# Six places for the split weights, and a reordered turn from the mixer into the feed-forward part, in a decoder layer on one core

## The chip, the cores and the metric

The kernel runs on one core of a Trainium2 chip. The metric is the device time of one execution in microseconds; less is better.

## The reference, cut to what matters

One layer of a decoder with 256 tokens of width 1024, in float32:

```
h = RMSNorm(x);  columns = h @ w_in          # 1024 x 5400: queries, keys, values, three merge gates
three attention branches -> o_nsa, o_moba, o_mem
merged = sum_i sigmoid(gate_i) * (o_i @ w_i)
y  = merged @ w_mix_out
x1 = x + RMSNorm(y)
h2 = RMSNorm(x1)
out = x1 + RMSNorm((silu(h2 @ w_gate) * (h2 @ w_up)) @ w_down)     # width 2816
```

## The kernel before, in words

Every projection is made from float32 values cut into a high and a low part. A product of two such values takes three matmuls: high times high, high activations times low weights, low activations times high weights. The weights are cut on the chip. They arrive in `raw` (four slots of 1 MB, one slot is one *unit*), and each half of a unit is one *sub*, numbered v. For each sub ScalarE (ACT) rounds 128x1024 values into `wh` (`hi`, L467) and VectorE (DVE) subtracts to get `wl` (`lo`, L756). Then TensorE (PE) runs 12 matmuls of 512 columns on it (`sub`, L1126): two token tiles t, two slices s of the contraction, three products (L1122 to L1124), into the PSUM bank pair `acc` of one block. Four subs make a block, `V_GATE`, `V_NSA`, `V_MIX`, `V_GU` and `V_DOWN` are the first subs of the stages, and `B_...` are the blocks.

`wh` and `wl` have four places (`SUBS`). So `hi` of sub v waits until the matmuls of sub v-4 are done (`mm_done`), and ACT's and DVE's programs name a lead of three subs (`AHEAD`): before each other piece of work they write `hi_to(v_last + AHEAD)` and `lo_to(...)`, which emit all splits up to that sub. The queues of the engines run in the order of the program, so a split that waits holds what stands behind it. The SP engine only issues the loads of `raw`; a slot is free when its two `lo` are done.

The stages in order are: five projection blocks and the memory block (the front); the loop over 24 attention *jobs* (`for n in range(JOBS + 2)`), which gives each job a gate sub, scores, a softmax through ACT, DVE and GpSimd (POOL), `turn` (transposes of the probabilities) and `values`; the output projections of the branches; the blocks `B_MIX` and `B_MIX + 1`, which are the two column halves of `merged @ w_mix_out`; the 11 blocks of gate and up; and down.

Around the change the work is serial by nature. The merged values `yb` come out of DVE (L949); PE transposes them in banks of four 128x128 blocks (`merged_banks`, two banks a call), ACT rounds a bank into `xh` (`round_hi(2, j)`, L506), and DVE makes `xl` (`round_lo(2, j)`, L798). Sub i of `B_MIX` needs bank i. After `B_MIX + 1` each token tile t goes through: sum of squares (ACT L672), root (L518), reciprocal (DVE L1037), two residual adds of 512 columns (`add_residual`, L1044, each gives `x1_done[n]`), transposes of the new x (`new_x_bank(t, n)`, L1202), `round_hi(3, 2t + n)` on ACT (L500) and `round_lo(3, 2t + n)` on DVE (L791), which give `th_done` and `tl_done`. The first feed-forward block `B_GU` is run by `by_tiles`: all of tile 0, then all of tile 1, and each pair of subs waits for `tl_done`, which is the low part. The square of the new x for the second norm (L696) comes after all roundings, for both tiles at once, followed by the load of the Silu table (L700).

Of the kernel before, what the change touches and what calls it, by code (L numbers as in the profile page):

```python
# [25 lines left out]
F32 = mybir.dt.float32  # L26
# [31 lines left out]
RAW, SUBS = 4, 4  # L58
AHEAD = SUBS - 1
# [6 lines left out]
V_GATE, V_MOBA, V_MEM, V_GATE_NSA, V_NSA, V_MIX, V_GU, V_DOWN = 24, 40, 42, 44, 52, 56, 2 * U_GU, 2 * U_DOWN  # L66

# [43 lines left out]

def look_ahead(n):

    return AHEAD - 1 if n < 6 else AHEAD


def build_layer(nc, a, out, g_scratch):
# [13 lines left out]
    with ExitStack() as ctx:  # L131
# [77 lines left out]
        with late:  # L209
            ah = sb("ah", [P, KF, SEQ], F32R, late)  # L210
            al = sb("al", [P, KF, SEQ], F32R, late)
            yb = sb("yb", [P, TILES, D], F32, late)
            tmp = sb("tmp", [P, TILES, SLICE], F32, late)
# [239 lines left out]
        def _(act):  # L453
# [7 lines left out]
            def hi(v, slot, half, w, first_load):  # L461

                act.wait_ge(loaded[slot], first_load)
                if not (isinstance(v, int) and v < SUBS):
                    act.wait_ge(mm_done, v - SUBS + 1)
                k = (2 * slot + half) % SUBS
                nc.scalar.activation(wh[:, k, :, 0:w], raw[:, slot, 2 * half:2 * half + 2, 0:w], ACT.Copy).then_inc(hi_done, 1)  # L467

            def first_hi(k):
# [7 lines left out]
                nc.scalar.activation(wh[:, k // 2, k % 2], raw[:, k // 4, k % 4], ACT.Copy).then_inc(hi_done, 1)  # L477

            def hi_to(v_end):
                while split[0] <= min(v_end, 2 * UNITS - 1):  # L480
                    v = split[0]
                    u = v // 2
                    hi(v, u % RAW, v % 2, width(v), 32 * (u // RAW + 1))
# [40 lines left out]
            split[0] = SUBS  # L524
# [11 lines left out]
            def evac_cols(b):  # L536
                v_last = 4 * b + 3
                hi_to(v_last + AHEAD)
# [90 lines left out]
            for n in range(JOBS + 2):  # L629
                hi_to(V_GATE + n + AHEAD)  # L630
# [47 lines left out]
            hi_to(V_MIX + 7)  # L678
# [3 lines left out]
            hi_to(V_GU + 1)  # L682
            round_hi(3, 0)
            hi_to(V_GU + 2)
# [16 lines left out]

            def ffn_hi(i, j, s):

                v = V_GU + AHEAD + s + 4 * i
                vj = AHEAD + s + 4 * j
                hi(v, (vj // 2) % RAW, vj % 2, SLICE, ((V_GU + vj) // 2 // RAW + 1) * 32 + (i - j) * 16)
# [6 lines left out]
            def ffn_act(i, j, first):  # L713
                for s in range(4):
                    if not first:
                        ffn_hi(i, j, s)
                    if s == 2 and not first:
# [12 lines left out]
            ffn_act(0, 0, True)  # L730
            with nc.scalar.Fori(0, (GU_BLOCKS - 1) // 2) as it:
                for j in range(2):
                    ffn_act(it * 2 + (1 + j), 1 - j, False)
            split[0] = V_GU + 4 * GU_BLOCKS + AHEAD
            hi_to(V_DOWN + 2 + AHEAD)
            ffn_ah(GU_BLOCKS - 1)
            nc.scalar.preload_act_table(ACT.Sqrt)
            for n in range(2):
                v_last = V_DOWN + 11 * n + 10
                hi_to(v_last + AHEAD)  # L740
# [8 lines left out]
        def _(dve):  # L749
            split = [0]  # L750

            def lo(v, slot, half, w):

                dve.wait_ge(hi_done, v + 1 + SUBS)
                k = (2 * slot + half) % SUBS
# [3 lines left out]
            def first_lo(k):  # L759

                dve.wait_ge(hi_done, k + 1)
                nc.vector.tensor_tensor(wl[:, k // 2, k % 2], raw[:, k // 4, k % 4], wh[:, k // 2, k % 2].bitcast(F32),
                                        ALU.subtract).then_inc(lo_done, 1)

            def lo_to(v_end):
                while split[0] <= min(v_end, 2 * UNITS - 1):
                    v = split[0]
                    lo(v, v // 2 % RAW, v % 2, width(v))
# [51 lines left out]
            split[0] = SUBS  # L820
# [18 lines left out]
            def evac_cols(b):  # L839
                v_last = 4 * b + 3  # L840
                lo_to(v_last + AHEAD)
# [210 lines left out]
            lo_to(V_MIX + 7)  # L1052
# [17 lines left out]
            lo_to(V_GU + AHEAD + 3)  # L1070
            dve.wait_ge(root_done, 5)
            reciprocals(3, 3)
            dve.wait_ge(rstd_done, 5)

            def ffn_lo(i, j, s):
                vj = AHEAD + s + 4 * j
                lo(V_GU + AHEAD + s + 4 * i, (vj // 2) % RAW, vj % 2, SLICE)
# [6 lines left out]
            def ffn_dve(i, j, first):  # L1084
                for s in range(4):
                    if not first:
                        ffn_lo(i, j, s)
                    if s == 2 and not first:
# [8 lines left out]
            ffn_dve(0, 0, True)  # L1097
            with nc.vector.Fori(0, (GU_BLOCKS - 1) // 2) as it:
                for j in range(2):
                    ffn_dve(it * 2 + (1 + j), 1 - j, False)  # L1100
            split[0] = V_GU + 4 * GU_BLOCKS + AHEAD
            lo_to(V_DOWN + 2 + AHEAD)
            ffn_al(GU_BLOCKS - 1)
            dve.wait_ge(gpostd, 32)
            lo_to(V_DOWN + 10 + AHEAD)
# [12 lines left out]
        def _(pe):  # L1118
# [7 lines left out]
            def sub(v, slot, parity, h, l, k0, w, first, last):  # L1126

                pe.wait_ge(lo_done, v + 1 + SUBS)
                for t in range(TILES):
# [3 lines left out]
                    if t == 0 and last:  # L1133
                        ins.then_inc(acc0_done, 1)
                ins.then_inc(mm_done, 1)
# [8 lines left out]
            def whole_block(b, v0, subs, h, l, k0=0, w=SLICE, ready=None, after=None):  # L1144
# [3 lines left out]
                for i in range(subs):  # L1148
                    if ready is not None:
                        ready(i)  # L1150
                    sub(v0 + i, (v0 + i) % SUBS, b % 2, h, l, k0 + 2 * i, w, i == 0, i == subs - 1)
# [3 lines left out]
            def first_block(after):  # L1155

                for k in range(PIECES):
                    slot, s = k // 2, k % 2
# [16 lines left out]
            def by_tiles(b, v0, subs, h, l, k0, ready=None, after=None, first=True):  # L1175
# [3 lines left out]
                for t in range(TILES):  # L1179
                    for i in range(subs):  # L1180
                        v = v0 + i
                        if t == 0:
                            pe.wait_ge(lo_done, v + 1 + SUBS)
# [327 lines left out]
```

## Time and profile before

| what | value |
|---|---|
| median of 3 runs | 421.06 us (418.35 to 421.47) |
| the profiled execution | 418.43 us, its span 416.6 us |
| PE busy | 408.3 us, 98% of the span |
| DVE / ACT / POOL busy | 260.9 / 234.0 / 32.1 us |
| granted TensorE clock | 1.00 in this execution |
| moved by DMA | 78.82 MB, mean 189 GB/s |

A busy share counts a matmul from its start to its modelled end, and these overlap. So the share doesn't show a short bubble; the distance from one start to the next does.

### The profile page before, as it was taken

How to read it: one execution, taken by the hardware profiler on the slowest of the kernel's cores; microseconds unless marked ns; L12 is line 12 of the kernel's file. 1: busy time of each engine (PE TensorE's matmuls, PEld its weight loads, DVE VectorE, ACT ScalarE, POOL GpSimd, SP SyncE). 2: the span in 40 equal slices, each digit the busy share in tenths (PEclk: the TensorE clock that was granted, in tenths of full speed). 3: DMA queues.
4: the chain of work that ended last, by engine and by line, in shares of the span. 5: the costliest groups of instructions: out<-in, count | busy, mean ns of one | idle time of the engine just before them, and what ended most of it. 6: DMA issues, size and time to landing. Idle time of an engine off the chain costs nothing.

```text
span 416.6 us, 5880 instructions
## 1 busy us (share of the span) xinstructions
PE 408.3 (98%) x2070; PEld 328.6 (79%) x2070; DVE 260.9 (63%) x454; ACT 234.0 (56%) x402; POOL 32.1 (8%) x72
## 2 busy tenths in 40 slices
PE   9999999999999999999999999999999999999994
PEld 5787789877777777778787788888888888888883
DVE  4854865875766789756859665555555655545434
ACT  5653964577767766745546774444554454545321
POOL 3210020021212121210000000000000000000000
PEclk9999999999999999999999999999999999999999
DMA  8999993535344335367654467555655556655002
GB/s 295 392 335 368 376 338 114 192 108 196 109 151 146 101 102 169 136 220 238 198 178 171 132 225 229 169 173 189 201 187 168 170 183 199 202 203 197 6 0 101
DMA packets 52016, 78.82 MB, mean 189 GB/s; under 512 B 2076, under 2 KB 28488, under 8 KB 51992
## 3 DMA queue, kind: packets, MB, share of 16 engines
q1 hardware_dynamic: 50216, 73.52, 53.4%
q0 software_dynamic: 1344, 4.43, 3.2%
q10 hardware_dynamic: 432, 0.56, 0.4%
q8 instruction: 14, 0.23, 0.2%
q14 instruction: 10, 0.08, 0.1%
HBM read 77.43 MB, written 1.07 MB: 188 GB/s over the span
## 4 chain that ended last, share of the span: by engine, by line
PE 96%; DVE 1%; ACT 1%; issue 1%; DVEq 0%; ACTq 0%
PE acc L1122 27%; PE acc L1124 27%; PE acc L1123 27%; PE ob L1363 3%; PE sbank L1312 3%; PE ptb L1326 2%; PE ptb L1445 1%; PE ptb L1282 1%; PE acc L1161 1%; PE acc L1165 1%; PE acc L1166 1%; PE sbank L1233 1%; DVE xl L791 1%; ACT xh L500 0%; PE ob L1249 0%
## 5 line engine op out<-in xcount | busy, mean ns | idle before, releaser
L756 DVE TENSOR_TENSOR wl<-raw,wh 128x1024 fp32r<-128x1024 f32 (+1 forms) x126 | 151.4, 1208 | 94.8 <-ACT wh L467 94.3
L467 ACT ACTIVATE wh<-raw 128x1024 fp32r<-128x1024 f32 (+1 forms) x126 | 130.9, 1045 | 91.3 <-PE acc L1124 79.4
L1122 PE MATMUL acc<-wh,xh 128*128 128x512 f32 (+1 forms) x368 | 146.2, 397 | 1.2 <-DVE xl L791 1.2
L1124 PE MATMUL acc<-wh,xl 128*128 128x512 f32 (+1 forms) x368 | 142.2, 387 | 0.0
L1123 PE MATMUL acc<-wl,xh 128*128 128x512 f32 (+1 forms) x368 | 142.0, 386 | 0.0
L1122 PEld LDWEIGHTS acc<-wh,xh 128*128 128x128 f32 x368 | 69.1, 188 | 18.1 <-issue 4.9
L1124 PEld LDWEIGHTS acc<-wh,xl 128*128 128x128 f32 x368 | 69.1, 188 | 14.2
L1123 PEld LDWEIGHTS acc<-wl,xh 128*128 128x128 f32 x368 | 69.2, 188 | 12.6
L1122 PE MATMUL acc<-wh,ah 128*128 128x512 f32 x88 | 34.3, 390 | 0.0
L1124 PE MATMUL acc<-wh,al 128*128 128x512 f32 x88 | 34.3, 389 | 0.0
L1123 PE MATMUL acc<-wl,ah 128*128 128x512 f32 x88 | 34.2, 389 | 0.0
L440 POOL TENSOR_SCALAR sx<-sx,jst 128x256 f32<-128x256 f32 (+1 forms) x48 | 20.3, 436 | 94.4 <-DVE jst L991 52.6
L642 ACT ACTIVATE sx<-sx,jst 128x128 f32<-128x128 f32 (+1 forms) x40 | 17.9, 450 | 8.1 <-DVE jst L981 8.1
L1122 PEld LDWEIGHTS acc<-wh,ah 128*128 128x128 f32 x88 | 16.5, 188 | 3.4
L1123 PEld LDWEIGHTS acc<-wl,ah 128*128 128x128 f32 x88 | 16.5, 188 | 3.4
L1124 PEld LDWEIGHTS acc<-wh,al 128*128 128x128 f32 x88 | 16.5, 188 | 3.4
L726 ACT ACTIVATE silu<-acc,rstd 128x256 f32<-128x256 f32 x22 | 10.4, 476 | 11.8 <-DVE act_tok L1094 8.0
L971 DVE TENSOR_TENSOR sx<-sbank,tb 128x128 f32<-128x128 f32 (+1 forms) x40 | 12.4, 352 | 5.2 <-PE sbank L1312 4.3
L1094 DVE SCALAR_TENSOR_TENSOR act_tok<-acc,rstd,silu 128x256 f32<-128x256 f32 x22 | 10.5, 480 | 6.8 <-ACT silu L726 6.8
L620 ACT ACTIVATE pts<-ptb 128x512 f32<-128x512 f32 x16 | 9.5, 597 | 9.0 <-PE ptb L1326 8.9
L1122 PE MATMUL acc<-wh,oh 128*128 128x512 f32 x32 | 13.0, 405 | 0.0
L672 ACT ACTIVATE tmp<-acc 128x512 f32<-128x512 f32 x8 | 4.8, 600 | 14.2 <-PE acc L1124 14.2
(187 smaller groups left out, 401.7 us busy)
## 6 DMA issues: line engine op xcount, KB each, us to landing
raw<-in_w_in SPq DMA_DIRECT2D x18, 1024.0 KB
raw<-in_w_ffn_gate SPq DMA_DIRECT2D x22, 512.0 KB
raw<-in_w_ffn_up SPq DMA_DIRECT2D x22, 512.0 KB
raw<-in_w_ffn_down SPq DMA_DIRECT2D x22, 512.0 KB
raw<-in_w_mix_out SPq DMA_DIRECT2D x4, 1024.0 KB
raw<-in_w_mem_kv SPq DMA_DIRECT2D x2, 1024.0 KB
raw<-in_w_nsa_o SPq DMA_DIRECT2D x2, 1024.0 KB
raw<-in_w_in SPq DMA_DIRECT2D x3, 512.0 KB, 7.4
```

The costliest lines, as they stand in the source:

```text
L440: ins = nc.gpsimd.tensor_scalar(sx[:, n % 2, lo:hi], sx[:, n % 2, lo:hi], jst[:, 4, n, t:t + 1], 1.0, ALU.mult, ALU.mult)
L467: nc.scalar.activation(wh[:, k, :, 0:w], raw[:, slot, 2 * half:2 * half + 2, 0:w], ACT.Copy).then_inc(hi_done, 1)
L642: ins = nc.scalar.activation(sx[:, n % 2, lo:hic], src[:, n % 2, lo:hic], ACT.Exp, bias=jst[:, 1, n, t:t + 1], scale=SCALE, accum_out=jst[ ...
L726: nc.scalar.activation(silu[:, t], acc[:, j % 2, t, 0:GU_W], ACT.Silu, scale=rstd[:, 3, t:t + 1]).then_inc(silu_done, 1)
L756: nc.vector.tensor_tensor(wl[:, k, :, 0:w], raw[:, slot, 2 * half:2 * half + 2, 0:w], wh[:, k, :, 0:w].bitcast(F32), ALU.subtract).then_in ...
L971: nc.vector.tensor_tensor(sx[:, n % 2, c0:c1], sbank[:, n % 2, c0:c1], tb[:, bh, c1 - c0 - 1::-1], ALU.add).then_inc(dve_c, 1)
L1094: nc.vector.scalar_tensor_tensor(act_tok[:, t], acc[:, j % 2, t, GU_W:2 * GU_W], rstd[:, 3, t:t + 1], silu[:, t], ALU.mult, ALU.mult).then ...
L1122: nc.tensor.matmul(bank[:, 0:w], h[:, k, c], wh[:, slot, s, 0:w], start=first, stop=False)
L1123: nc.tensor.matmul(bank[:, 0:w], h[:, k, c], wl[:, slot, s, 0:w], start=False, stop=False)
L1124: return nc.tensor.matmul(bank[:, 0:w], l[:, k, c], wh[:, slot, s, 0:w], start=False, stop=last)
L1312: ins = nc.tensor.matmul(sbank[:, side, c0:c1], qt[half_rows(side), q, P * t:P * t + P], kt[half_rows(side), k, 0:c1 - c0], start=True, st ...
L1363: ins = nc.tensor.matmul(ob[half_rows(side), c0:c1], v, p, start=(i == 0), stop=(i == count - 1))
```

## The change

It has four parts.

1. `wh` and `wl` get six places. A sub's place is now `ring(v)`, and `hi` waits for the last user of that place, v-6, up to the first feed-forward blocks. The lead stays at three in the front, grows to five over the first jobs, and goes back to four places and three subs from feed-forward block 3 on. For that, feed-forward blocks 1 and 2 are taken out of ACT's and DVE's loops and written out, with fewer splits in them. In the front, after block 1, the splits that are emitted ahead of the copy out of the bank go to sub 9 and not to sub 10.
2. In `B_MIX` the second pair of merged banks is turned in the middle of sub 1 (after its tile 0), and not after sub 0.
3. `B_GU` is written out as `first_ffn_block`. The two products with the high part of the new x run first for a pair of subs, and the product with the low part after them. The high products wait for `th_done` only. The transposes of tile 1 stand after `high(0, 2)` and after `high(1, 0)`.
4. The squares of the new x are made per tile, each ahead of the rounding of one bank of tile 1. On DVE the first residual add of tile 1 now comes before `round_lo(3, 1)`.

The buffer `tmp` shares its memory with `silu` and `act_tok` to make room.

```diff
-RAW, SUBS = 4, 4
-AHEAD = SUBS - 1
+RAW, SUBS, FFN_SUBS, IN_PIECES = 4, 6, 4, 4
+FRONT_AHEAD, AHEAD, FFN_AHEAD = 3, SUBS - 1, FFN_SUBS - 1
+FFN_PARTS = [[V_GU + 9, V_GU + 10, V_GU + 11, V_GU + 12], [V_GU + 13, V_GU + 14]]
+def ring(v):
+    w = v - V_GU
+    return w % SUBS if w < 2 * SUBS else w % FFN_SUBS
+def last_user(v):
+    return v - SUBS if v - V_GU < 2 * SUBS + FFN_SUBS else v - FFN_SUBS
 def look_ahead(n):
-    return AHEAD - 1 if n < 6 else AHEAD
+    return min(AHEAD, max(FRONT_AHEAD - 1, n - 1))
+def hi_look_ahead(n):
+    return min(AHEAD, max(FRONT_AHEAD, n))
+def front_look_ahead(b):
+    return FRONT_AHEAD - 1 if b == 1 else FRONT_AHEAD
...
 # ACT
-                hi_to(v_last + AHEAD)
+                hi_to(v_last + front_look_ahead(b))
...
-                hi_to(V_GATE + n + AHEAD)
+                hi_to(V_GATE + n + hi_look_ahead(n))
...
-            hi_to(V_MIX + 7)
+            hi_to(V_GU + 1)
             squares(0, 1, 0, B_MIX + 1, V_MIX + 7)
             act.wait_ge(sum_done, 1)
             roots(2, 0, 1)
-            hi_to(V_GU + 1)
+            hi_to(V_GU + 3)
             round_hi(3, 0)
-            hi_to(V_GU + 2)
+            hi_to(V_GU + 4)
             squares(0, 1, 1, B_MIX + 1, V_MIX + 7)
             round_hi(3, 1)
             act.wait_ge(sum_done, 2)
             roots(2, 1, 2)
-            hi_to(V_GU + 3)
-            for j in (2, 3):
-                round_hi(3, j)
-            hi_to(V_GU + AHEAD + 3)
-            for n in range(2):
-                act.wait_ge(x1_done[n], 2)
+            hi_to(V_GU + 5)
+            def x_squares(t):
+                for n in range(2):
+                    act.wait_ge(x1_done[n], t + 1)
+                nc.scalar.activation(yb[:, t], xs[:, t], ACT.Square, accum_out=ssq[:, 3, t:t + 1]).then_inc(ssq_done, 1)
             for t in range(TILES):
-                nc.scalar.activation(yb[:, t], xs[:, t], ACT.Square, accum_out=ssq[:, 3, t:t + 1]).then_inc(ssq_done, 1)
+                x_squares(t)
+                round_hi(3, 2 + t)
             act.wait_ge(ssq_done, 6)
             roots(3)
+            hi_to(V_GU + AHEAD + 3)
             nc.scalar.preload_act_table(ACT.Silu)
...
 # DVE
-            lo_to(V_GU + 1)
+            lo_to(V_GU + 3)
             round_lo(3, 0)
-            lo_to(V_GU + 2)
+            lo_to(V_GU + 4)
             sum_halves(0, 1)
             gain(0, 1, 1, B_MIX)
-            round_lo(3, 1)
             norm(1, 4, 2, 4)
             add_residual(0, 1, 0, 2, x1_done)
-            lo_to(V_GU + 3)
+            round_lo(3, 1)
             add_residual(0, 1, 1, 2, x1_done)
-            for j in (2, 3):
-                round_lo(3, j)
-            lo_to(V_GU + AHEAD + 3)
+            round_lo(3, 2)
+            lo_to(V_GU + 5)
+            round_lo(3, 3)
             dve.wait_ge(root_done, 5)
             reciprocals(3, 3)
+            lo_to(V_GU + AHEAD + 3)
...
 # PE
             whole_block(B_MIX, V_MIX, 4, xh, xl, ready=lambda i: pe.wait_ge(tl_done, i + 1),
-                        after={0: [lambda: merged_banks(2, 4)]})
+                        between={1: lambda: merged_banks(2, 4)})
...
-            by_tiles(B_GU, V_GU, 4, xh, xl, 0, ready=4, after={(0, 2): [lambda: new_x_bank(1, 0)], (0, 3): [lambda: new_x_bank(1, 1)]})
+            def first_ffn_block():
+                def high(t, i):
+                    pe.wait_ge(th_done, 4 + 2 * t + i // 2 + 1)
+                    if t == 0:
+                        pe.wait_ge(lo_done, V_GU + i + 1 + IN_PIECES)
+                    for s in range(2):
+                        x = xh[:, 2 * i + s, P * t:P * t + P]
+                        nc.tensor.matmul(acc[:, B_GU % 2, t], x, wh[:, i, s], start=(i == 0 and s == 0), stop=False)
+                        nc.tensor.matmul(acc[:, B_GU % 2, t], x, wl[:, i, s], start=False, stop=False)
+                def low(t, i):
+                    pe.wait_ge(tl_done, 4 + 2 * t + i // 2 + 1)
...
+                for i in range(2):
+                    high(0, i)
+                for i in range(2):
+                    low(0, i)
+                high(0, 2)
+                new_x_bank(1, 0)
+                high(0, 3)
+                low(0, 2)
+                low(0, 3)
+                for half in range(2):
+                    for i in (2 * half, 2 * half + 1):
+                        high(1, i)
+                        if i == 0:
+                            new_x_bank(1, 1)
+                    for i in (2 * half, 2 * half + 1):
+                        low(1, i)
```

## Rows read from the trace of the kernel before

**Rows 1.** The page, section 1: busy time of the engines.

```profile
PE 408.3 (98%) x2070; PEld 328.6 (79%) x2070; DVE 260.9 (63%) x454; ACT 234.0 (56%) x402; POOL 32.1 (8%) x72
```

**Rows 2.** Busy time by stretch: the jobs, then the feed-forward loop; granted clock, DMA share, GB/s.

```profile
84.00:184.00 100.00, 100.00 (x578) 76.81 (x577) 72.84 (x186) 67.59 (x154) 20.80 (x48) 1.00 0.43 138
250.00:350.00 100.00, 100.00 (x460) 82.75 (x459) 56.13 (x61) 49.11 (x61) 0.00 (x0) 1.00 0.60 187
```

**Rows 3.** The waits of PE: us in total, times, longest.

```profile
PE acc L1122 <- DVE xl L791: 1.2, 2, 0.7
...
PE ptb L1207 <- DVE yb L949: 0.2, 1, 0.2
```

**Rows 4.** The timeline at `B_MIX`: start, duration, engine, line, operation, idle before.

```profile
201.77 0.39 PE L1124 MATMUL acc<-wh,xl 128*128 128x512 f32 x1
...
202.40 0.66 PE L1207 MATMUL ptb<-const,yb 128*128 128x128 f32 x4 [0.25 <-DVE yb L949]
...
203.25 0.48 PE L1122 MATMUL acc<-wh,xh 128*128 128x512 f32 x1
...
203.79 0.76 DVE L798 SCALAR_TENSOR_TENSOR xl<-ptb,xh 128x256 fp32r<-128x256 f32 x2 [0.30 <-ACT xh L506]
```

**Rows 5.** The timeline of PE at the end of `B_MIX + 1`, in `B_GU`, and the start of block 1.

```profile
223.08 0.39 PE L1124 MATMUL acc<-wh,xl 128*128 128x512 f32 x1
...
224.14 0.47 PE L1122 MATMUL acc<-wh,xh 128*128 128x512 f32 x1 [0.68 <-DVE xl L791]
...
230.36 0.60 PE L1202 MATMUL ob<-const,xs 128*128 128x128 f32 x4
...
231.44 0.50 PE L1122 MATMUL acc<-wh,xh 128*128 128x512 f32 x1 [0.48 <-DVE xl L791]
...
237.00 0.39 PE L1122 MATMUL acc<-wh,xh 128*128 128x512 f32 x1
```

**Rows 6.** The timeline of ACT in the same stretch.

```profile
221.70 1.14 ACT L500 ACTIVATE xh<-sbank,gx 128x128 fp32r<-128x128 f32 x4 [0.69 <-PE sbank L1202]
...
224.23 1.17 ACT L500 ACTIVATE xh<-sbank,gx 128x128 fp32r<-128x128 f32 x4
...
236.86 1.04 ACT L696 ACTIVATE yb<-xs 128x1024 f32<-128x1024 f32 x1
...
239.38 1.28 ACT L700 ACT_TABLE_LOAD   x1
```

**Rows 7.** The timeline of DVE in the same stretch.

```profile
222.87 1.12 DVE L791 SCALAR_TENSOR_TENSOR xl<-sbank,gx,xh 128x128 fp32r<-128x128 f32 x4 [0.43 <-ACT xh L500]
...
226.94 0.75 DVE L1044 SCALAR_TENSOR_TENSOR xs<-yb,rstd,xs 128x512 f32<-128x512 f32 x1
...
228.74 0.75 DVE L1044 SCALAR_TENSOR_TENSOR xs<-yb,rstd,xs 128x512 f32<-128x512 f32 x1
```

**Rows 8.** The timeline in the front: the first transposes, then sub 12.

```profile
32.38 0.41 PE L1233 MATMUL sbank<-const,pat 128*128 128x128 f32 x2 [0.42 <-issue]
...
39.72 1.06 ACT L467 ACTIVATE wh<-raw 128x1024 fp32r<-128x1024 f32 x1 [5.12 <-DMA raw<-in_w_in]
...
40.81 1.23 DVE L756 TENSOR_TENSOR wl<-raw,wh 128x1024 fp32r<-128x1024 f32 x1 [5.83 <-ACT wh L467]
...
42.19 0.47 PE L1122 MATMUL acc<-wh,xh 128*128 128x512 f32 x1
```

**Rows 9.** The timeline in jobs 4 and 5.

```profile
93.47 1.07 ACT L467 ACTIVATE wh<-raw 128x1024 fp32r<-128x1024 f32 x1
...
96.23 0.93 POOL L440 TENSOR_SCALAR sx<-sx,jst 128x256 f32<-128x256 f32 x2 [3.25 <-DVE jst L994]
...
98.46 0.48 ACT L642 ACTIVATE sx<-sbank,jst 128x256 f32<-128x256 f32 x1
...
99.14 0.60 PE L1326 MATMUL ptb<-const,sx 128*128 128x128 f32 x4
...
101.11 1.13 PE L1312 MATMUL sbank<-kt,qt 64*128 64x256 f32 x8
```

More of the change, by code:

```diff
@@ L212, in build_layer @@
             yb = sb("yb", [P, TILES, D], F32, late)
-            tmp = sb("tmp", [P, TILES, SLICE], F32, late)
+            with ExitStack() as early:
+                tmp = sb("tmp", [P, TILES, SLICE], F32, early)
             silu = sb("silu", [P, TILES, GU_W], F32, late)
@@ L476, in first_hi @@
                     act.wait_ge(loaded[k // 4], 32)
-                nc.scalar.activation(wh[:, k // 2, k % 2], raw[:, k // 4, k % 4], ACT.Copy).then_inc(hi_done, 1)
+                nc.scalar.activation(wh[:, ring(k // 2), k % 2], raw[:, k // 4, k % 4], ACT.Copy).then_inc(hi_done, 1)
             def hi_to(v_end):
@@ L523, in _ @@
                 first_hi(k)
-            split[0] = SUBS
+            split[0] = IN_PIECES
             def squares_of(i, src, t):
@@ L711, in ffn_ah, with ffn_act @@
                 nc.scalar.activation(ah[:, bass.ds(i * 2, 2), :], ptb[:], ACT.Copy).then_inc(ah_done, 1)
-            def ffn_act(i, j, first):
+            def ffn_act(i, j, first, parts=None):
                 for s in range(4):
-                    if not first:
+                    if parts is None:
                         ffn_hi(i, j, s)
+                    elif s < len(parts):
+                        hi_to(parts[s])
                     if s == 2 and not first:
@@ L819, in _ @@
                 first_lo(k)
-            split[0] = SUBS
+            split[0] = IN_PIECES
             dve.wait_ge(bias_row, 1)
@@ L1082, in ffn_al, with ffn_dve @@
                                         ah[:, bass.ds(i * 2, 2), :].bitcast(F32), ALU.subtract).then_inc(al_done, 1)
-            def ffn_dve(i, j, first):
+            def ffn_dve(i, j, first, parts=None):
                 for s in range(4):
-                    if not first:
+                    if parts is None:
                         ffn_lo(i, j, s)
+                    elif s < len(parts):
+                        lo_to(parts[s])
                     if s == 2 and not first:
@@ L1124, in product, with sub @@
                 return nc.tensor.matmul(bank[:, 0:w], l[:, k, c], wh[:, slot, s, 0:w], start=False, stop=last)
-            def sub(v, slot, parity, h, l, k0, w, first, last):
-                pe.wait_ge(lo_done, v + 1 + SUBS)
+            def sub(v, slot, parity, h, l, k0, w, first, last, between=None):
+                pe.wait_ge(lo_done, v + 1 + IN_PIECES)
                 for t in range(TILES):
@@ L1134, in sub @@
                         ins.then_inc(acc0_done, 1)
+                    if t == 0 and between is not None:
+                        between()
                 ins.then_inc(mm_done, 1)
@@ L1142, in free_acc, with whole_block @@
                     pe.wait_ge(ev[t], b - 1)
-            def whole_block(b, v0, subs, h, l, k0=0, w=SLICE, ready=None, after=None):
+            def whole_block(b, v0, subs, h, l, k0=0, w=SLICE, ready=None, after=None, between=None):
                 free_acc(b)
@@ L1150, in whole_block @@
                         ready(i)
-                    sub(v0 + i, (v0 + i) % SUBS, b % 2, h, l, k0 + 2 * i, w, i == 0, i == subs - 1)
+                    sub(v0 + i, ring(v0 + i), b % 2, h, l, k0 + 2 * i, w, i == 0, i == subs - 1, (between or {}).get(i))
                     for work in (after or {}).get(i, ()):
@@ L1414, in _ @@
                 free_acc(b)
-                sub(v, v % SUBS, b % 2, oh, ol, 4, SLICE, True, False)
+                sub(v, ring(v), b % 2, oh, ol, 4, SLICE, True, False)
                 if n == 0:
@@ L1426, in _ @@
-            by_tiles(B_GU, V_GU, 4, xh, xl, 0, ready=4, after={(0, 2): [lambda: new_x_bank(1, 0)], (0, 3): [lambda: new_x_bank(1, 1)]})
+            def first_ffn_block():
[9 more added lines that the diff above has]
+                    pe.wait_ge(tl_done, 4 + 2 * t + i // 2 + 1)
+                    for s in range(2):
+                        ins = nc.tensor.matmul(acc[:, B_GU % 2, t], xl[:, 2 * i + s, P * t:P * t + P], wh[:, i, s], start=False,
+                                               stop=(i == 3 and s == 1))
+                    if t == 1:
+                        ins.then_inc(mm_done, 1)
+                    elif i == 3:
+                        ins.then_inc(acc0_done, 1)
+                for i in range(2):
[14 more added lines that the diff above has]
+                        low(1, i)
@@ L1447, in ffn_turn_at @@
                 ins.then_inc(at_done, 1)
+            free_acc(B_GU)
+            first_ffn_block()
             ffn_body(1, 1, True)
```

76 lines of the change are left out of this document (39 added, 37 removed).

## The prediction

> **What bounds the kernel now.** I read the busy times first: PE has 98% of the span, and DVE and ACT have a third or more of theirs free [rows 1]. Then I asked by stretch: in the jobs and in the feed-forward loop PE is covered for the whole 100 us at a granted clock of 1.00 (the 2.4 GHz level), DMA engines are at 43% and 60% of their time, and DVE has at least 27 us of every 100 free [rows 2]. So the time is the number of PE instructions times their spacing, plus the bubbles. The change removes no PE instruction; it can only take bubbles. The spacing is worked out from rows 5: from the first matmul of tile 1 of `B_GU` at 231.44 to the first of the next block at 237.00 there are 24 matmuls, 5.56 us; the first after transposes lasts 0.50 and not 0.39 and costs those 0.11 more, so one takes (5.56 - 0.11) / 24 = 0.227 us. A full share in a busy column hides bubbles, so the view that matters is that of PE's own waits. It is short: 1.2 us in two waits for the low part of the new x, and 0.2 us for the merged values [rows 3]. No wait of PE for a split weight (`wh`, `wl`) is in that view, in the jobs or after them.
>
> **The bubbles and their sizes**, as start minus previous start minus the normal spacing:
>
> - `B_MIX`: the last matmul of sub 0 starts at 201.77, the transposes at 202.40: 0.63 - 0.23 = 0.40 us [rows 4].
> - `B_GU`, tile 0: from 223.08 to 224.14, 1.06 - 0.23 = 0.83 us [rows 5].
> - `B_GU`, tile 1: the four transposes start at 230.36, the next matmul at 231.44. Eight transposes held PE from 202.40 to 203.25 [rows 4], so four take 0.43 us, and the bubble is 1.08 - 0.43 = 0.65 us [rows 5].
> - The front: PE's sequencer idles 0.42 us ahead of the transposes at 32.38 [rows 8].
>
> The first three add up to 1.88 us, or 0.45% of the span.
>
> **Part by part.**
>
> *Merged banks amid sub 1: takes 0.40 us.* Sub 0 now ends at 201.77 + 0.23 = 202.00, and six matmuls of sub 1 run until 203.36. `yb` was there for transposes at 202.40, so they don't wait. Then eight transposes (0.85), then six more matmuls with 0.11 of restart: sub 2 wants to start at 203.36 + 0.85 + 1.47 = 205.68. It needs `xl` of bank 2, which came at 203.79 + 0.76 = 204.55, that is 2.15 us after the first transpose [rows 4]; now 203.36 + 2.15 = 205.51. The margin is 0.17 us. If it is missed, the loss is at most 0.3 us.
>
> *High parts first: takes 0.83 us.* With the 0.40 from above, `B_MIX + 1` ends at 223.31 - 0.40 = 222.91. The rounding of bank 0 ended at 221.70 + 1.14 = 222.84 [rows 6], now 222.44, so the high products don't wait. Eight of them last until 224.72. The low part of bank 0 came at 222.87 + 1.12 = 223.99 [rows 7], now 223.59, so the low products don't wait either (to 225.63). The high part of bank 1 came at 224.23 + 1.17 = 225.40 [rows 6], now 225.0: margin 0.6 us.
>
> *Transposes of tile 1 and order on DVE: takes 0.65 us.* After `high(0, 2)` PE is at 226.54 and wants `x1_done[0]` of tile 1. Its add started at 226.94 and took 0.75 [rows 7], but one `round_lo` (1.12) stood before it, which now stands behind: 227.69 - 0.40 - 1.0 = 226.3. Margin 0.25 us. The transposes (226.54) are followed by four high and four low products (to about 228.9). ACT meanwhile has the root, one split (1.07), one `x_squares` (1.04 [rows 6]) and `round_hi(3, 2)` (1.14): 225.1 + 1.07 + 1.04 + 1.14 = 228.35. Margin 0.55 us. The second half of the chain is looser: the add of the other columns, with `round_lo(3, 1)` before it, is done near 228.0 (it ended at 229.49 [rows 7]) for transposes at 229.8; `round_hi(3, 3)` is done near 231.5 for 232.2. So I have PE through `B_GU` at 222.91 + 48 x 0.227 + 2 x (0.43 + 0.10) = 234.9, where it was 237.0 [rows 5]. That is 2.1 us; the three bubbles give 1.88, the rest is the slow restart behind each of them. I take 2.0.
>
> *Squares per tile.* Two operations of 1.04 us that stood at 236.86 to 238.9, ahead of the 1.28 us table load at 239.38 [rows 6], now run inside the block. ACT's last splits before the table are bound to PE's subs 0 to 2 of `B_GU`; the third is done at about 235.6, the table at 236.9, Silu of block 0 after it. PE asks for the products two subs into block 1 (234.9 + 5.4 = 240.3). Covered by 2 us; worth nothing by itself.
>
> *Six places.* In the steady state `hi(v)` stands one lead further on and waits for v-6, so it is the same event of PE as before (lead 3, v-4; lead 5, v-6: both are the sub before the current one). ACT and DVE do the same work at the same moments, and only PE's distance grows, by two subs or 5.4 us. PE didn't wait for weights [rows 3], so this gives nothing. It costs where the lead grows: jobs 4 and 5 each have one more `hi` (1.07 us [rows 9]) and, around them, one more `lo` (1.23 us [rows 8]) ahead of the softmax steps. The slack there: POOL's scaling of job 4 ended at 96.23 + 0.93 = 97.16, and PE's transposes of it start at 99.14, so 2.0 us, of which one `hi` takes 1.1. The exponentials of job 5 end at 98.46 + 0.48 = 98.94, and the next scores overwrite their bank at 101.11, so 2.2 us, of which two `hi` take 2.1 less the 0.7 that ACT waited in between: about 1 us is left [rows 9]. The extra splits therefore lie beside PE's work; bounds 0 and, if `hi` and `lo` add up in series, 2 x 2.3 = 4.6 us less the slacks 2.0 + 2.2, so 0.4 us, or 4.6 us if no slack holds. I take 0. A load of `raw` is asked for seven subs ahead of its use both before and after, as both ends move together; the DMA rows have room [rows 2]. Splits that the feed-forward blocks 1 and 2 no longer have were done before; nobody is short there. Code written out for two blocks on ACT and DVE: no row prices it; between 0 and one idle of PE like the 0.42 us of rows 8. I take 0, as those engines are a third free.
>
> At this place the Trainium skill, SBUF — State Buffer, section "SBUF: two separate sides", has a rule against the change: a VectorE operation with two SBUF inputs and a GpSimd operation that reads SBUF shut each other out for a whole instruction. No row here shows POOL beside a `lo`, since POOL starts right after DVE's reciprocal. If an added `lo` did hold POOL in job 4, one of 1.23 us would outlast the 0.9 us of slack left by 0.3 us, and the sum would be 1.7 and not 2.0.
>
> *The front.* Copying block 1 out ahead of sub 10's split lets the transposes at 32.38 start without the 0.42 us idle. But sub 12 waits for its load: `hi` starts at 39.72 behind 5.12 us of waiting for DMA, `lo` ends at 40.81 + 1.23 = 42.04, and PE starts at 42.19 [rows 8]. That load doesn't depend on the splits, so PE arrives earlier and waits longer. Worth 0; up to 0.6 if the load comes earlier too.
>
> **The sum.** 418.43 - 2.0 = 416.4 for an execution like the profiled one (span 414.6; the rest of 1.8 us stays). The profiled one lies at the low end of the runs; the median is 421.06, and against it the forecast is 421.06 - 2.0 = **419.1 us**.
>
> **The rivals.**
>
> - *Part of it comes back* (0.14): the chain of tile 1 has margins of 0.17, 0.25 and 0.55 us. If DVE or ACT are late there by the length of one operation (1.1 us), PE waits at `new_x_bank(1, 0)` or `high(1, 0)`; 1.0 us is left, 420.1. For it: a chain of eight hand-overs. Against it: all durations are from rows.
> - *The lead covers late weights* (0.10): two of three runs took 3 us more than the profiled one, and no trace shows where. If it is a split or a load that comes late after the front, 5.4 us more distance hides it: 418.43 - 2.0 = 416.4 for every run. Against it: the tightest loads are in the front [rows 8], where the lead stays.
> - *The jobs pay* (0.08): in jobs 4 and 5 the added splits stand ahead of exponentials and reciprocals on queues in order. It decides once they delay POOL or the exponentials by more than the 2.0 and 2.2 us of slack. With no slack 4.6 us are lost and 2.0 won: 421.06 + 2.6 = 423.7, slower.
> - *It doesn't do what it says* (0.06): a wait in `B_GU` is inherited from elsewhere, and the freed time is lost before block 1: 421.1.
>
> The forecast itself has 0.62.
>
> **How the numbers follow.** About 1% (4.2 us) is what a measurement here can tell from no change, and the whole sum is half of that. Faster by over 1% needs under 416.9: the second rival and a share of the scatter, 0.10. Slower by over 1% needs over 425.3: only the far end of the third rival, 0.03. Within 1%: 0.87. The range reaches from 416.2 (second rival) to 420.9 (above the first rival, short of the fourth), which leaves out the third and fourth and a little of the scatter of 3 us between runs.
>
> **What would show it.** In the changed profile: PE's waits have no entry for `xl` in `B_GU` over 0.2 us and none for `yb`; first matmul of block 1 about 2 us earlier; the bubble at 32.38 gone and a larger one at 42.19; the squares of x between the roundings of tile 1; POOL and PE in jobs 4 and 5 as before within 0.3 us. It is wrong if PE stands in the new block for `x1_done` or `th_done`, or if a wait of PE turns up in the jobs.

## The result, and the profile after

| kernel | runs | median us | lowest to highest |
|---|---|---|---|
| before | 6 | 419.48 | 418.35 to 421.47 |
| changed | 6 | 416.27 | 416.18 to 416.33 |

The ratio is 0.9915, with a 95% interval of 0.9888 to 0.9942: the change takes 0.85%. The few long runs of the kernel before weigh in the ratio and hardly in a median; the ratio of the medians is 0.9923. The profiled execution took 416.27 us with a span of 414.5 us, against 418.43 and 416.6. So trace against trace it takes 2.1 us, and median against median 3.2 us. Two things have to be explained: that the 2.1 us are where they were forecast, and that the scatter of the kernel before doesn't show in these six runs.

The changed kernel's page, busy time of the engines, and then its waits of PE (us in total, times, longest), which answer to [rows 1] and [rows 3]:

```profile
PE 407.3 (98%) x2070; PEld 328.2 (79%) x2070; DVE 260.6 (63%) x454; ACT 233.1 (56%) x402; POOL 32.9 (8%) x72
```

```profile
PE ptb L1314 <- DVE eps L838: 0.9, 1, 0.9
PE acc L1152 <- DVE wl L782: 0.4, 1, 0.4
PE acc L1193 <- ACT wh L498: 0.2, 1, 0.2
```

The waits for `xl` and for `yb` are gone. A new one for a split weight has come; it is at sub 12 in the front (below). The wait of 0.2 us at L1193 is in the first block, and the one at L1314 was there before. The timeline of the changed kernel at `B_MIX`, answering to [rows 4]:

```profile
203.24 0.39 PE L1154 MATMUL acc<-wh,xl 128*128 128x512 f32 x1
203.48 0.60 PE L1239 MATMUL ptb<-const,yb 128*128 128x128 f32 x4
...
204.27 0.48 PE L1152 MATMUL acc<-wh,xh 128*128 128x512 f32 x1
...
204.80 0.76 DVE L824 SCALAR_TENSOR_TENSOR xl<-ptb,xh 128x256 fp32r<-128x256 f32 x2 [1.21 <-ACT xh L527]
...
205.50 0.39 PE L1154 MATMUL acc<-wh,xl 128*128 128x512 f32 x1
...
205.73 0.40 PE L1152 MATMUL acc<-wh,xh 128*128 128x512 f32 x1
```

The last matmul of tile 0, the transposes and the next matmul follow each other with no idle time noted. From the last matmul of sub 1 at 205.50 to the first of sub 2 at 205.73 is 0.23, the normal spacing; `xl` of bank 2 was ready at 204.80 + 0.76 = 205.56.

`B_GU` in the same timeline, answering to [rows 5] and [rows 6]:

```profile
222.74 0.39 PE L1154 MATMUL acc<-wh,xl 128*128 128x512 f32 x1
...
222.97 0.40 PE L1466 MATMUL acc<-wh,xh 128*128 128x512 f32 x1
...
226.04 1.08 ACT L715 ACTIVATE yb<-xs 128x1024 f32<-128x1024 f32 x1
...
226.39 0.39 PE L1467 MATMUL acc<-wl,xh 128*128 128x512 f32 x1
226.62 0.60 PE L1234 MATMUL ptb<-const,xs 128*128 128x128 f32 x4
226.98 0.48 PE L1466 MATMUL acc<-wh,xh 128*128 128x512 f32 x1
...
227.26 1.14 ACT L521 ACTIVATE xh<-ptb,gx 128x128 fp32r<-128x128 f32 x4
...
228.91 0.40 PE L1466 MATMUL acc<-wh,xh 128*128 128x512 f32 x1
```

Where PE stood 0.83 us beyond its spacing there is now the spacing alone, 222.97 - 222.74 = 0.23. Tile 1's transposes start one spacing after the matmul before them, and hold PE for 226.98 - 226.62 = 0.36 us. `round_hi(3, 2)` ends at 227.26 + 1.14 = 228.40, and `high(1, 0)` starts at 228.91, right after the low products. Block 1 then starts here:

```profile
233.93 1.07 PE L1472 MATMUL acc<-wh,xl 128*128 128x512 f32 x4
...
234.84 0.39 PE L1152 MATMUL acc<-wh,xh 128*128 128x512 f32 x1
```

It was 237.00 [rows 5], so 2.16 us earlier, which is all of the difference of the spans (2.1). The front, answering to [rows 8]:

```profile
32.02 0.38 PE L1265 MATMUL sbank<-const,pat 128*128 128x128 f32 x2
...
39.69 1.06 ACT L488 ACTIVATE wh<-raw 128x1024 fp32r<-128x1024 f32 x1 [5.49 <-DMA raw<-in_w_in]
...
41.38 0.39 PE L1154 MATMUL acc<-wh,xl 128*128 128x512 f32 x1
...
42.16 0.47 PE L1152 MATMUL acc<-wh,xh 128*128 128x512 f32 x1 [0.38 <-DVE wl L782]
```

The bubble before the transposes is gone, the one at sub 12 is 42.16 - 41.38 - 0.23 = 0.55 us, and sub 12 starts at 42.16 where it was 42.19. Jobs 4 and 5, answering to [rows 9]:

```profile
93.44 2.02 ACT L488 ACTIVATE wh<-raw 128x1024 fp32r<-128x1024 f32 x2
...
97.14 0.93 POOL L462 TENSOR_SCALAR sx<-sx,jst 128x256 f32<-128x256 f32 x2 [4.19 <-DVE jst L1020]
...
98.00 2.35 DVE L782 TENSOR_TENSOR wl<-raw,wh 128x1024 fp32r<-128x1024 f32 x2
...
99.20 0.60 PE L1358 MATMUL ptb<-const,sx 128*128 128x128 f32 x4
...
101.19 0.49 PE L1344 MATMUL sbank<-kt,qt 64*128 64x256 f32 x2
```

Two splits stand where one stood. POOL starts 0.91 us later than at 96.23 [rows 9], and PE's transposes come at 99.20 where they came at 99.14.

### The profile page after: what moved, and what is told of

The parts are those of the page before. It is cut to its first block, busy times and chain, and to the rows that moved or that the text cites. A ratio compares the mean times of both kernels' runs of the same rounds, so it can differ in the third digit from the quotient of the medians.

```text
span 414.5 us, 5854 instructions
## 1 busy us (share of the span) xinstructions
PE 407.3 (98%) x2070; PEld 328.2 (79%) x2070; DVE 260.6 (63%) x454; ACT 233.1 (56%) x402; POOL 32.9 (8%) x72
## 4 chain that ended last, share of the span: by engine, by line
PE 89%; DMA 8%; SPq 1%; DVE 1%; ACT 1%; issue 0%; DVEq 0%
PE acc L1152 25%; PE acc L1154 25%; PE acc L1153 25%; DMA raw<-in_w_in 8%; PE ob L1395 3%; PE sbank L1344 3%; PE ptb L1358 2%; PE ptb L1514 1%; PE acc L1466 1%; PE acc L1467 1%; PE acc L1472 1%; ACT wh L488 0%; PE ob L1281 0%; PE ob L1307 0%; PE sbank L1265 0%; DVE wl L782 0%
## 5 line engine op out<-in xcount | busy, mean ns | idle before, releaser
L1152 PE MATMUL acc<-wh,xh 128*128 128x512 f32 (+1 forms) x352 | 139.6, 397 | 0.4 <-DVE wl L782 0.4
L1154 PE MATMUL acc<-wh,xl 128*128 128x512 f32 (+1 forms) x352 | 136.0, 386 | 0.0
L1153 PE MATMUL acc<-wl,xh 128*128 128x512 f32 (+1 forms) x352 | 135.7, 386 | 0.0
L1152 PEld LDWEIGHTS acc<-wh,xh 128*128 128x128 f32 x352 | 66.1, 188 | 16.0 <-issue 3.9
L1154 PEld LDWEIGHTS acc<-wh,xl 128*128 128x128 f32 x352 | 66.1, 188 | 13.6
L1153 PEld LDWEIGHTS acc<-wl,xh 128*128 128x128 f32 x352 | 66.2, 188 | 12.0
```

Of the source, the lines that this page charges most:

```text
L1152: nc.tensor.matmul(bank[:, 0:w], h[:, k, c], wh[:, slot, s, 0:w], start=first, stop=False)
L1153: nc.tensor.matmul(bank[:, 0:w], h[:, k, c], wl[:, slot, s, 0:w], start=False, stop=False)
L1154: return nc.tensor.matmul(bank[:, 0:w], l[:, k, c], wh[:, slot, s, 0:w], start=False, stop=last)
```

## The experiments

All are timed against the kernel before on the same chip: e0 to e3 on one, e4 to e7 on a second, e8 to e11 on a third. As above, long runs weigh in the ratio and hardly in the median, so the two columns differ a little.

| kernel | median us | lowest, highest | runs | ratio to before, 95% |
|---|---|---|---|---|
| e0, before again | 418.75 | 418.31, 419.50 | 12 | 0.9993 (0.9980 to 1.0007) |
| e1, places alone | 418.60 | 418.40, 420.03 | 12 | 0.9992 (0.9978 to 1.0006) |
| e2, order alone | 422.49 | 421.54, 425.47 | 6 | 1.0095 (1.0061 to 1.0129) |
| e3, front edit alone | 418.43 | 418.25, 418.70 | 12 | 0.9980 (0.9964 to 0.9995) |
| e4, changed, old front | 416.34 | 416.07, 417.33 | 6 | 0.9938 (0.9915 to 0.9960) |
| e5, order with a split moved | 417.03 | 416.61, 419.06 | 12 | 0.9958 (0.9943 to 0.9973) |
| e6, squares late | 416.41 | 416.17, 416.50 | 6 | 0.9934 (0.9913 to 0.9955) |
| e7, memory tokens later | 415.66 | 415.29, 416.20 | 6 | 0.9917 (0.9895 to 0.9940) |
| e8, before, late unit | 427.86 | 427.20, 428.54 | 5 | 1.0202 (1.0178 to 1.0226) |
| e9, front edit, late unit | 423.08 | 423.02, 424.58 | 5 | 1.0103 (1.0078 to 1.0129) |
| e10, banks after sub 0 | 416.63 | 416.53, 416.85 | 6 | 0.9941 (0.9921 to 0.9961) |
| e11, changed again | 416.41 | 416.17, 416.57 | 6 | 0.9934 (0.9914 to 0.9954) |

The runs of the kernel before beside the three groups had medians of 418.81 (29 runs, 418.22 to 421.46), 418.93 (17, 418.29 to 421.09) and 418.90 us (11, 418.27 to 421.26).

**Before, again.** 

> The kernel before, unchanged, run as a kernel of its own, to see its scatter and to get a second trace of it. If the scatter of 3 us belongs to the kernel before (some of its executions meet a bubble that the first trace does not show), its times spread again over 418.4 to 421.5 us, and a slower execution's trace shows the bubble. If it belonged to that chip or hour, all times lie within 0.5 us of 418.4 and the ratio is 1.000.

It spread by 1.2 us: it had no execution near 421 among its twelve. Its profiled execution took 418.96 us. Its timeline at the first transposes:

```profile
30.05 1.06 ACT L467 ACTIVATE wh<-raw 128x1024 fp32r<-128x1024 f32 x1 [4.84 <-DMA raw<-in_w_in]
...
32.28 0.75 DVE L851 TENSOR_SCALAR pat<-acc,rstd 128x512 f32<-128x512 f32 x1
...
33.13 0.41 PE L1233 MATMUL sbank<-const,pat 128*128 128x128 f32 x2 [1.49 <-issue]
```

Here is the small part of the scatter at work. The split of sub 10 waits for its load until 30.05; it was 29.30 in the first trace. The copies of block 1 stand behind it on ACT and DVE, and PE's transposes need both copies: 33.13 instead of 32.38, the same 0.75 us later. The idle time ahead is 1.49 us and not 0.42 [rows 8]. From there PE is late enough that sub 12 doesn't wait (it starts at 42.75 and not 42.19), and this trace's span is 0.6 us longer, that is 0.75 less the 0.17 us that sub 12 waited in the first.

**Front edit alone.**

```diff
 # in evac_cols of ACT and of DVE
-                hi_to(v_last + AHEAD)
+                hi_to(v_last + (AHEAD - 1 if b == 1 else AHEAD))
```

> The kernel before with one edit: after block 1 the splits go to sub 9, not sub 10, before the copy out of the bank. Theory of the bubbles: the 0.58 us bubble at the first transposes is gone and the one at sub 12 grows by as much; 0 us. If the scatter comes from late loads in the front, where this copy stands behind a split that waits for its load, this kernel has none or less of it: all times within 0.5 us of 418.4.

The scatter fell to 0.45 us in 12 runs, where the 12 of the kernel before above spread by 1.2 and the 29 by 3.2. The median fell by 0.38 us or 0.1%; in the ratio of 0.9980 the long executions of the kernel before weigh too, and its interval (0.9964 to 0.9995) leaves out 1 by little. The load of sub 10 came even later in its trace, at 30.54, and did no harm:

```profile
27.53 0.69 ACT L549 ACTIVATE pat<-acc,rstd 128x512 f32<-128x512 f32 x1 [2.41 <-PE acc L1124]
28.83 0.75 DVE L851 TENSOR_SCALAR pat<-acc,rstd 128x512 f32<-128x512 f32 x1 [2.08 <-PE acc L1124]
...
30.54 2.01 ACT L467 ACTIVATE wh<-raw 128x1024 fp32r<-128x1024 f32 x2 [2.32 <-DMA raw<-in_w_in]
...
42.12 0.47 PE L1122 MATMUL acc<-wh,xh 128*128 128x512 f32 x1 [1.00 <-DVE wl L756]
```

Both copies are over before the split. PE comes 1.0 us early to sub 12 and waits there for a load whose split starts at 39.5 to 39.9 in every trace that keeps the order of the loads.

**Places alone.** The changed kernel with `by_tiles(B_GU, ...)`, `after={0: ...}` for the banks, the squares after all roundings, and DVE's old order. 

> Part 1 alone: six places, lead of five, feed-forward blocks 1 and 2 written out, and the shorter lead in front of the copy of block 1; the turn of the merged banks, the first feed-forward block and the squares as before. Theory of the bubbles: 0 us against a fast execution of the kernel before, so 418.4, with the bubbles of 0.40, 0.83 and 0.65 still in the trace. Theory of the cover (late weights after the front make the scatter): its times lie within 0.3 us of each other near 418.4, while those of the kernel before spread to 421.

Within the interval it equals the kernel before, and it isn't faster than the front edit alone (418.60 against 418.43), which it holds. So six places and the lead of five give nothing by themselves, and the longer lead isn't what took the scatter. The traces even show a small cost: from sub 12 to the transposes of `B_MIX` PE takes 160.35 us here and 160.21 in the kernel before. One of the twelve runs took 420.03, 1.4 us over the median; no trace shows why.

**Order alone.** Parts 2 to 4 with four places, and the front as before.

```diff
-RAW, SUBS, FFN_SUBS, IN_PIECES = 4, 6, 4, 4
+RAW, SUBS, FFN_SUBS, IN_PIECES = 4, 4, 4, 4
 # and, on ACT and DVE, leads of three:
-            hi_to(V_GU + 5)
+            hi_to(V_GU + 3)
 # ... (the other leads too, and the splits of feed-forward blocks 1 and 2)
```

> Parts 2 to 4 alone: banks turned amid sub 1, high parts first, squares per tile, with four places and a lead of three throughout and the front as before. Theory of the bubbles: 2.0 us less than a fast execution of the kernel before, 416.4. Theory of the cover: the fastest at 416.4 too, but with the scatter of the kernel before, up to 3 us.

A miss by 6.1 us, the wrong way. The timeline, and then busy time by stretch (PE, PEld, DVE, ACT, POOL, granted clock, DMA share, GB/s):

```profile
226.52 0.60 PE L1234 MATMUL ptb<-const,xs 128*128 128x128 f32 x4
...
229.37 1.21 DVE L782 TENSOR_TENSOR wl<-raw,wh 128x1024 fp32r<-128x1024 f32 x1
230.73 0.76 PE L1466 MATMUL acc<-wh,xh 128*128 128x512 f32 x1 [3.61 <-DVE wl L782]
...
231.29 0.63 PE L1467 MATMUL acc<-wl,xh 128*128 128x512 f32 x1
231.71 0.63 PE L1466 MATMUL acc<-wh,xh 128*128 128x512 f32 x1
...
241.22 0.39 PE L1152 MATMUL acc<-wh,xh 128*128 128x512 f32 x1
```

```profile
226.50:230.70 4.20, 0.61 (x5) 0.36 (x4) 3.65 (x9) 2.78 (x8) 0.00 (x0) 0.88 0.43 138
230.70:237.00 6.30, 6.27 (x18) 4.99 (x19) 0.00 (x0) 0.13 (x1) 0.00 (x0) 0.54 0.52 168
237.00:245.00 8.00, 8.00 (x37) 6.62 (x36) 5.66 (x10) 7.15 (x12) 0.00 (x0) 1.00 0.22 61
```

`high(0, 3)` needs the low part of sub 3's weights. With four places I had put that subtraction on DVE behind `round_lo(3, 2)`, which hangs on the transposes of tile 1: 3.61 us of idle PE. After the idle the granted clock fell to about half (0.54 over the stretch), and matmuls came every 0.43 us (231.29 to 231.71) and not 0.23. From 230.73 to 235.98 there are 12; at 0.227 with one restart they take 2.83, so the clock cost 5.25 - 2.83 = 2.4 us. The transposes behind them took 0.61 and not 0.36, 0.25 more. Counted from start to start, as the other bubbles, the bubble is 230.73 - 226.52 - 0.36 = 3.85 us. That makes 6.5 us, and the trace bears it out: from the first matmul of `B_GU` (222.86) to that of block 1 (241.22) it takes 18.36 us, and the changed kernel 234.84 - 222.97 = 11.87.

**Order, with that split moved.**

```diff
 # DVE, against the kernel above
             add_residual(0, 1, 0, 2, x1_done)
+            lo_to(V_GU + 3)
             round_lo(3, 1)
             add_residual(0, 1, 1, 2, x1_done)
             round_lo(3, 2)
-            lo_to(V_GU + 3)
             round_lo(3, 3)
```

> Parts 2 to 4 with four places and a lead of three, and on DVE the low part of sub 3 of the first feed-forward block made before the low part of bank 1, not after bank 2. Theory that the 3.6 us wait comes from the place of that split in DVE's queue, and that six places matter only because they let it go earlier: high(0, 3) waits at most 1 us, low(0, 2) at most 0.7 us, and the time is 416.5 to 417.8, below the kernel before. Theory that the new block needs the lead of five in any order: it stays above 418.8.

At 417.03 us it is below the kernel before. PE's wait for the split weight is 0.4 us in its trace (0.61 from start to start), and the clock holds:

```profile
227.66 0.47 PE L1466 MATMUL acc<-wh,xh 128*128 128x512 f32 x1 [0.37 <-DVE wl L782]
```

So four places do for the new block. Six are worth the rest: sub 3's split is then done long before, and out of the way of the chain of tile 1. Against the changed kernel with the same old front (416.34, next) that is 0.7 us. Their traces agree: from the transposes of `B_MIX` to block 1 one takes 235.55 - 203.54 = 32.01 us and the other 234.64 - 203.28 = 31.36, 0.65 less.

**Changed, old front.**

```diff
-    return FRONT_AHEAD - 1 if b == 1 else FRONT_AHEAD
+    return FRONT_AHEAD
```

> The changed kernel with the one front edit undone: the splits go to sub 10 again before the copy of block 1. Theory of the front (the copy stands behind a split whose load lands at a moment that differs from run to run): the scatter is back, fastest 416.3, median 416.7 or more, some executions up to 3 us longer, and in the trace the bubble is at the first transposes. Theory of the bubbles alone: 416.3 with no scatter, as the changed kernel.

The median is that of the changed kernel within 0.1 us. The spread is 1.3 us against 0.15 and 0.4 for the changed kernel's two sets of six. Its trace had an early load (split of sub 10 at 29.15) and the bubble at the first transposes. So of the two theories neither is shown by these six: one run lies 1.0 us over the median, and the median, which I had expected at 416.7 or more, didn't move. The next pair was made for it.

**The late unit, twice.** In the kernel before, and in the one with the front edit alone:

```diff
-            projection(2)
+            plain(4, w_in, 0, SLICE * 2)
+            sp.dma_start(memt0[:], memt).then_inc(memtd, 16)
+            plain(5, w_in, 4, SLICE * 2)
             sp.wait_ge(grow_done, 2)
             sp.dma_start(g_scratch, grow[:]).then_inc(g_stored, 16)
-            sp.dma_start(memt0[:], memt).then_inc(memtd, 16)
```

> The kernel before with the second unit of block 2 (subs 10 and 11) made late on purpose: the memory tokens (1 MB, 2.8 us at 370 GB/s) are loaded ahead of it and not after it; the unit for sub 12 stands where it stood. Theory of the front: in the kernel before, the copy of block 1 stands behind that unit's split, so the first transposes start near 35.2 instead of 32.4 and the kernel takes 2.6 us more (2.8 less the 0.17 that sub 12 waits anyway): 421 us, as in the slowest executions. If the scatter has another cause, 418.8.

> The same late unit, in the kernel before with the one front edit (copy of block 1 ahead of the split of sub 10). Theory of the front: the transposes start at 31.5 all the same, sub 10 is needed only near 34.5 and sub 12 still waits for its load until 42.1: 418.4. Otherwise 421 like its twin.

The unit came later than I had worked out: in the first of the two the split of sub 10 started at 36.84, 7.5 us late and not 2.8, so neither number holds. The difference between the twins does the work: 427.86 - 423.08 = 4.8 us for one edit. PE in the first and in the second:

```profile
39.92 0.66 PE L1234 MATMUL sbank<-const,pat 128*128 128x128 f32 x2 [7.90 <-issue]
```

```profile
39.29 0.50 PE L1123 MATMUL acc<-wh,xh 128*128 128x512 f32 x1 [3.56 <-DVE wl L757]
...
40.32 0.56 PE L1124 MATMUL acc<-wl,xh 128*128 128x512 f32 x1
40.68 0.63 PE L1125 MATMUL acc<-wh,xl 128*128 128x512 f32 x1
41.10 0.63 PE L1123 MATMUL acc<-wh,xh 128*128 128x512 f32 x1
```

Without the edit PE idles 7.9 us at the first transposes, after sub 8; with it PE does them and sub 9, and idles 3.6 us where the late weights themselves are needed, at sub 10. In both the clock halves after the bubble: in the second the spacing goes to 0.42 from 40.68 on, and in the first the stretch after it has a granted clock of 0.50:

```profile
40.00:45.00 5.00, 5.00 (x14) 4.10 (x15) 3.80 (x6) 2.55 (x5) 0.52 (x1) 0.50 1.04 399
```

The direction that I expected is shown, the sizes are not: the late unit costs 9.0 us without the edit (427.86 against 418.90) and 4.7 with it (423.08 against the 418.43 of the front edit alone), so the edit hides about half.

**Squares late.** The changed kernel, with the loop over `x_squares(t)` after the one over `round_hi(3, 2 + t)`. 

> The changed kernel with the squares of both tiles after both roundings, as they were before. My own working: covered by 2 us, so 416.3 within 0.2 us. A rival: roots and Silu come 1 to 2 us later and PE waits for the products of block 0 at its turn in block 1, up to 1 us more.

416.41 us, as the changed kernel run again: squares per tile are covered either way and worth nothing. From sub 12 to block 1 its trace takes 192.69 us, the changed kernel's 192.68.

**Banks after sub 0.** The changed kernel with `after={0: [lambda: merged_banks(2, 4)]}` for `between={1: ...}`. 

> The changed kernel with the merged banks turned after sub 0, as before. The bubble of 0.40 us is back at that place: 416.27 + 0.40 = 416.7. If the turn amid sub 1 merely moved the wait, 416.3.

416.63 against 416.41 of the changed kernel on the same chip, with traces of 414.8 and 414.7. The bubble is back in its trace at the same place, with 202.43 - 201.79 - 0.23 = 0.41 us, and the medians differ by 0.2 us; 416.27 of the first six runs would make it 0.36. The traces settle the size: from the start of sub 12 to that of block 1 this one takes 235.19 - 42.05 = 193.14 us, the next one 235.04 - 42.33 = 192.71. The bubble costs 0.43 us, and the rest of the difference lies in the front, where PE's start at sub 12 moves with its load.

**Changed, again.** 

> The changed kernel again, on the chip of the other three: 416.3 with a scatter under 0.5 us if the change takes the sensitivity of the front away; over 1 us of scatter if its first six runs were only lucky.

416.17 to 416.57. In this trace the bubble at sub 12 is 1.04 us, the split there starts at 39.86 and not 39.69, and the end comes 0.2 us later, as the split does.

**Memory tokens later: a version that beats both.**

```diff
-            sp.dma_start(memt0[:], memt).then_inc(memtd, 16)
-            projection(3)
+            plain(6, w_in, 0, SLICE * 3)
+            sp.dma_start(memt0[:], memt).then_inc(memtd, 16)
+            plain(7, w_in, 4, SLICE * 3)
```

> The changed kernel with the transposed memory tokens (1 MB) loaded after the first unit of block 3, not before it. Theory of the front: PE's arrival at sub 12 is set by that unit's load (split at 39.7, PE at 42.16 after a bubble of 0.55 us); it lands about 1 MB earlier, 2.8 us at 370 GB/s, the bubble goes, and the time is 415.7. If the load isn't what PE waits for, or the memory block then waits for its own input, 416.3 or more.

```profile
36.68 1.06 ACT L489 ACTIVATE wh<-raw 128x1024 fp32r<-128x1024 f32 x1 [2.51 <-DMA raw<-in_w_in]
...
38.39 0.60 PE L1266 MATMUL sbank<-const,pat 128*128 128x128 f32 x4
```

Sub 12's split starts at 36.68 and not 39.69, 3.0 us earlier, PE's waits have no entry for a split weight any more, PE starts sub 12 at 41.58 and not 42.16, and the time is 415.66: 0.6 us less than the changed kernel, the size of its bubble at sub 12. This also shows that the load of that unit paced PE there.

## Why the prediction was right in the trace and wrong in the level

**The bound and the three bubbles: right.** The three places, 0.40, 0.83 and 0.65 us, are empty in the changed trace. I had block 1 at 234.9 and it started at 234.84; the profiled time was forecast as 416.4 and was 416.27. The margins held too: bank 2 of `B_MIX` came 205.73 - 205.56 = 0.17 us before its use (forecast 0.17). The high part of bank 2 of the new x came 0.51 us before its use (forecast 0.55). One term was a little off: I gave four transposes 0.43 us, half of eight, and they hold PE 0.36, so the third bubble was 0.72 and not 0.65 us. Of the three places only that of `B_MIX` was put back by itself (0.43 us); the other two are shown by the timelines and, together, by the sum of 2.1.

**Six places: right alone, wrong in company.** "PE didn't wait for weights [rows 3], so this gives nothing" holds for the places alone (418.60 us, and 0.1 us of cost in the trace). But the step priced the places against the old order. In the new order the rounding chain of tile 1 and the splits of subs 3 to 5 fight for DVE, and the places decide that: 0.7 us if the four-place queue is ordered well, 6 us if it isn't. The term should have been priced with the other parts in place. It isn't what made the level miss, as the sum of the whole change came out in the trace.

**The jobs: right in the price, wrong in a sign.** The added splits delayed POOL by 0.91 us, where I had written "as before within 0.3 us", and PE by 0.06: the slack took the delay. At this place I had named the Trainium skill's rule on the shared port (SBUF — State Buffer, "SBUF: two separate sides"). POOL's two operations took 0.93 us as before, but they ran from 97.14 to 98.07 and the subtractions from 98.00, so they were hardly side by side: no run here tests the rule.

**Squares per tile: right**, by the late version.

**The step that failed: 421.06 - 2.0 = 419.1.** I took a gain worked out on an execution with an early load off a median that held late ones. Two terms of it are wrong.

*The base, 421.06.* It was a median of three, two of which were long. Over the 57 runs beside the experiments the kernel before lies at 418.8 to 418.9 in the median, so 2.2 us of the error of 419.1 - 416.3 = 2.8 in the level are this term.

*The front, "worth 0; up to 0.6".* I took this from one trace in which PE reached sub 12 0.17 us early, so that all it wins before would go into the wait there. That trace was an execution with an early load. In the next trace of the same kernel the load came 0.75 us later, the copy, the transposes and the end moved with it, and it cost 0.6 us; with the edit a load that came 1.2 us later than in the first trace cost nothing (the split of sub 10 at 30.54 against 29.30). So the edit is worth nothing where the load is early, the lateness beyond 0.17 us where it is a little late, 0.4 us on the median of the kernel before (418.81 to 418.43), and 4.8 us when the load is 7.5 us late. In the changed kernel its worth on the median isn't shown: without it the six runs have 416.34, with it 416.27 and 416.41. So of the 0.6 us of the error that the base leaves, 0.1 is the trace (2.1 for 2.0); the rest has the size of the front term, and that it is this term stays open.

The rival that named late data had the number, 416.4 for every run, but by luck: it looked for the late data after the front, where the lead grows, and the places alone are no faster than the front edit alone. What is shown is in the front, and what hides it is the order of a copy and a split, not a lead.

**The chances.** The ratio came out within 1%, which had 0.87. But I wrote that about 1% is what can be told from no change, and the changed kernel's first six runs lie within 0.15 us, 0.04%. Both its intervals, 0.9888 to 0.9942 and 0.9914 to 0.9954, leave out 1, so 0.87 for "within 1%" hid that the forecast was a plain gain. The 416.9 that I had set for "faster by over 1%" hung on the base of 421.06; the measured 416.27 lies below it and is still within 1% of the kernel before as measured.

**What stays open.** The two traces of the kernel before are of executions of 418.43 and 418.96 us; none was had of one that took over 420.4 us (7 of 63). Of 93 executions with the old front (the kernel before, e0, e4, e5) 22 took over 0.5 us more than their kernel's median and 8 over 1 us more; of 54 with the new front (the changed kernel, e1, e3, e6, e7, e10, e11) 2 and 1, that one being the 420.03 of e1. (e2 is left out, as its clock falls besides.) That fits the late load, and the twins show that a late load does such a thing; that it was the cause in those eight is argued, not shown, and e1's long run says that the new front doesn't take every one.

## What to carry to other kernels

A queue in program order couples things that have nothing to do with each other: before one operation is written ahead of another, ask whether the first waits for a transfer, whose moment differs from run to run, and what behind it PE needs. When one execution is profiled and the runs scatter, compare the trace's own time with the scatter first, and take a difference from like executions only; an edit that is free in the profiled execution can be worth something in the others. Price buffers and order together: a place more is worth what it lets you move out of the critical chain.

## What the runs showed that I had not expected

- The granted clock after a bubble. After 3.6 us of idle PE in e2 the clock fell to its lower level (matmuls of 512 columns every 0.43 us and not 0.23) for some 6 us, and the bubble cost 6.5 us in all. After 7.9 us of idle in the front (e8) it was the same: 0.50 over 40 to 45 us. In e9 it fell only 1 us after the bubble of 3.6 us, and for some 3.5 us. The bubble of 1.5 us in the second trace of the kernel before left the spacing at 0.23.
- Moving a load of 1 MB ahead of another of the same size delayed the second by 7.5 us, not by the 2.8 us of its bytes at 370 GB/s (the kernel before moves 374 GB/s from 20 to 25 us). SP's rows show that the second load's issue was over at 14.52 + 4.67 = 19.19 us and not at 10.48 + 4.38 = 14.86, so 4.3 of the 7.5 us are there before it is on its way. Several loads are under way together: the memory tokens took 20.6 us from issue to landing. So the landing isn't given by the order and the bytes alone; where the other 3.2 us come from stays open.
